# Differential attention: the difference of the two probability maps is made before the turning and the value product

## The reference, cut to what matters

```python
    def attend_block(args):
        qb, b_idx = args
        q_pos = b_idx * Q_BLOCK + jnp.arange(Q_BLOCK)
        logits = jnp.einsum('bhmqd,bhmkd->bhmqk', qb, k).astype(jnp.float32)
        bias = table[t5_bucket_3(key_pos[None, :] - q_pos[:, None])]
        logits = logits + jnp.transpose(bias, (2, 0, 1))[None, :, None]
        visible = key_chunk[None, :] <= (q_pos // CHUNK)[:, None]
        logits = jnp.where(visible, logits, -jnp.inf)
        p = jax.nn.softmax(logits, axis=-1)
        w = p[:, :, 0] - lam * p[:, :, 1]
        return jnp.einsum('bhqk,bhkv->bhqv', w.astype(v.dtype), v)
...
    o = rms_norm_3(o, out_norm_g) * (1.0 - lam_init)
    return o.reshape(B, S, H * 2 * d)
```

## Time and profile before

| | us |
|---|---|
| median of 3 runs | 2302.87 |
| lowest, highest | 2302.66, 2303.80 |
| the profiled execution's own time | 2307.78 |
| its span in the profile | 2306.0 |
| TensorE busy in the span | 1948.8 (85%) |
| VectorE busy | 622.1 (27%) |
| ScalarE busy | 289.0 (13%) |
| GpSimd busy | 101.6 (4%) |

### The profile page before, as it was taken

How to read it: one execution, slowest core, us unless ns; L and a number is a source line. 1 busy time by engine, 2 the same in 40 slices (tenths; PEclk the granted TensorE clock), 3 DMA queues, 4 the chain that set the end, 5 groups by cost and what they waited for, 6 DMA issues and landing times.

```text
span 2306.0 us, 30479 instructions
## 1 busy us (share of the span) xinstructions
PE 1948.8 (85%) x12705; PEld 1147.9 (50%) x12705; DVE 622.1 (27%) x1708; ACT 289.0 (13%) x742; POOL 101.6 (4%) x164
## 2 busy tenths in 40 slices
PE   8999999898655665799966566669999999999999
PEld 4455557554222222486533223224668854548874
DVE  3643583531000000122200000013625411334430
ACT  1123412421000000101100000001500001300000
POOL 0200002300000000000000000002200000010000
PEclk9999999999888888899987877879999999999999
DMA  9968395249999999975999999998234444324420
GB/s 357 386 248 318 121 360 199 64 177 414 425 426 426 426 426 426 370 221 212 380 425 427 426 426 427 425 416 283 72 111 152 164 141 146 110 74 156 163 101 18
DMA packets 194047, 636.81 MB, mean 276 GB/s; under 512 B 7473, under 2 KB 92737, under 8 KB 161448
## 3 DMA queue, kind: packets, MB, share of 16 engines
q1 hardware_dynamic: 187072, 623.78, 69.8%
q0 software_dynamic: 2528, 6.99, 0.9%
q10 hardware_dynamic: 4360, 4.83, 0.7%
HBM read 632.15 MB, written 1.09 MB: 275 GB/s over the span
## 4 chain that ended last, share of the span: by engine, by line
PE 65%; DMA 33%; DVE 1%; ACT 1%; issue 1%; POOL 0%; SPq 0%; DVEq 0%; ACTq 0%; POOLq 0%
DMA ring<-in_moe_w_down 32%; PE bank L713 17%; PE bank L696 17%; PE bank L2826 7%; PE bank L2287 4%; PE bank L1203 3%; PE bank L798 2%; PE bank L2478 1%; PE bank L2271 1%; PE bank L2189 1%; PE bank L2782 1%; PE bank L764 1%; PE bank L789 1%; PE bank L1094 1%; PE bank L610 1%; PE bank L1666 1%
## 5 line engine op out<-in xcount | busy, mean ns | idle before, releaser
L2271 PE MATMUL bank<-ring,arena 128*32 128x256 f32 x3968 | 306.8, 465 | 178.9 <-DMA ring<-in_moe_w_up 114.4
L2271 PEld LDWEIGHTS bank<-ring,arena 128*32 128x32 f32 x3968 | 140.0, 129 | 332.9 <-DMA ring<-in_moe_w_up 148.1
L696 PE MATMUL bank<-ring,hT 128*128 128x512 f32 (+2 forms) x704 | 296.1, 578 | 4.1 <-DVE hT L2466 2.9
L713 PE MATMUL bank<-xn,ring 128*128 128x256 f32 x1280 | 276.6, 379 | 0.0
L713 PEld LDWEIGHTS bank<-xn,ring 128*128 128x128 f32 x1280 | 243.2, 190 | 33.1
L2287 PE MATMUL bank<-ring,arena 128*32 128x256 f32 x1984 | 158.7, 475 | 84.1 <-DMA ring<-in_moe_w_down 73.0
L696 PEld LDWEIGHTS bank<-ring,hT 128*128 128x128 f32 x704 | 132.7, 191 | 154.2 <-issue 149.3
L2826 PE MATMUL bank<-ring,arena 128*128 128x512 f32 x352 | 151.6, 592 | 0.0
L2287 PEld LDWEIGHTS bank<-ring,arena 128*32 128x32 f32 x1984 | 71.8, 131 | 157.0 <-DMA ring<-in_moe_w_down 88.6
L2080 DVE TENSOR_TENSOR arena<-arena,bank 128x256 f32<-128x256 f32 x32 | 13.5, 421 | 491.8 <-ACT arena L2141 491.8
L713 PE MATMUL bank<-hT,ring 128*128 128x256 f32 x512 | 114.4, 386 | 2.0 <-ACT hT L2352 2.0
(11 more groups left out here) (445 smaller groups left out, 1828.0 us busy)
## 6 DMA issues: line engine op xcount, KB each, us to landing
ring<-in_moe_w_gate SPq DMA_DIRECT2D x62, 2048.0 KB, 26.4
ring<-in_moe_w_up SPq DMA_DIRECT2D x62, 2048.0 KB, 26.1
ring<-in_moe_w_down SPq DMA_DIRECT2D x62, 2048.0 KB, 26.2
ring<-in_ada_w SPq DMA_DIRECT2D x24, 2048.0 KB, 17.2
ring<-in_w_up SPq DMA_DIRECT2D x44, 1024.0 KB, 7.4
ring<-in_w_in SPq DMA_DIRECT2D x11, 2048.0 KB, 16.8
ring<-in_w_down SPq DMA_DIRECT2D x10, 2048.0 KB, 7.8
ring<-in_w_out SPq DMA_DIRECT2D x6, 2048.0 KB, 15.1
```

Of the source, the lines that this page charges most:

```text
L696: ins = t_.matmul(bank[b][:, 0:n], lhsT(k)[:, P * t:P * t + P], w[:, k, c0:c0 + n], start=(k == 0), stop=(k == kt - 1))
L713: ins = t_.matmul(bank[b][:, 256 * (j % 2):256 * (j % 2) + 256], w[:, k, P * j:P * j + P], rhs[:, k, :], start=(k == order[0]), stop=(k == ...
L2271: ins = t_.matmul(bank[4][32 * j:32 * j + 32, at:at + 256], xs_now[b][:, 4 * (c % 2) + k, :], w(k)[:, 256 * j:256 * j + 256], start=(c % 2 ...
```

## The change

Two units of a head are now handled together, as one pair s of 12. Both exponentials are taken as before. Then VectorE makes the combined map: the reciprocals of both row sums in one instruction (L2969), the second map scaled by its reciprocal and by minus lambda in place (L2971), and the first map scaled by its reciprocal and added to it (L2973). The last two work in SBUF on 128 or 256 columns, and each of the three waits for the one before. TensorE turns only the combined map (L2920) and makes one value product (L2929). ScalarE copies the product to the output with no factor (L2958), where VectorE had two instructions with factors. Four slots for biased scores and exponentials take the place of three. The first tile's sum and norms are hung into steps 9 and 11 to 13 of 14, where they stood in 17 and 20 to 22 of 27. GpSimd's squares wait for ScalarE's output.

```diff
--- before.py
+++ after.py
@@ -876,7 +876,7 @@
                     f = one_over(j) if u["factor"] is None else weight(j)
                     v.wait_ge(*dve_s.after(f"{tag}.r{j}" if u["factor"] is None else f"{tag}.f{j}"))
                     if u["add"]:
-                        v.wait_ge(*dve_s.after(f"{tag}.o{j - 1}" if tag == "diff" else f"{tag}.o{j - 2}"))
+                        v.wait_ge(*dve_s.after(f"{tag}.o{j - 2}"))
                     v.wait_ge(*pe_s.after(f"{tag}.pv{j}"))
                     src = bank[j % 2][:, 0:u["dst"].shape[-1]]
                     if u["add"]:
@@ -2895,11 +2895,97 @@
         diff_ss = [stats[:, at:at + 12] for at in (16, 40, 64)]
         diff_gain = small[:, 384:512]
 
+        DIFF_PAIRS = len(diff_units) // 2
+        diff_p, diff_s = (b[:, :, :].rearrange("p a (b c) -> p (a b) c", c=S) for b in (p_buf, s_buf))
+
+        def difference_pe(before):
+
+
+            t_ = nc.tensor
+            waits(t_, *before)
+            claim(0, 1, 2, 3, 4, 5, 6, 7)
+            for s in range(DIFF_PAIRS + 2):
+                if s < DIFF_PAIRS:
+                    if s >= 2:
+                        t_.wait_ge(*dve_s.after(f"diff.s{2 * s - 3}"))
+                    for i in (2 * s, 2 * s + 1):
+                        u = diff_units[i]
+                        t_.matmul(score_bank(i, FOUR)[:, 0:u["keys"]], u["q"], u["k"], start=True, stop=True).then_inc(*pe_s.signals(f"diff.qk{i}"))
+                if 1 <= s <= DIFF_PAIRS:
+                    g = s - 1
+                    t_.wait_ge(*dve_s.after(f"diff.c{g}"))
+                    if g >= 2:
+                        t_.wait_ge(*act_s.after(f"diff.pt{g - 2}"))
+                    for k in range(diff_units[2 * g]["keys"] // P):
+                        ins = t_.transpose(bank[6 + g % 2][:, P * k:P * k + P], diff_p[:, 2 * (g % 2), P * k:P * k + P], ident)
+                    ins.then_inc(*pe_s.signals(f"diff.T{g}"))
+                if s >= 2:
+                    g = s - 2
+                    t_.wait_ge(*act_s.after(f"diff.pt{g}"))
+                    if g >= 2:
+                        t_.wait_ge(*act_s.after(f"diff.o{g - 2}"))
+                    values = diff_units[2 * g]["v"]
+                    for k, v in enumerate(values):
+                        ins = t_.matmul(bank[g % 2][:, 0:P], pT_buf[:, g % 2, P * k:P * k + P], v, start=(k == 0), stop=(k == len(values) - 1))
+                    ins.then_inc(*pe_s.signals(f"diff.pv{g}"))
+            for g in (DIFF_PAIRS - 2, DIFF_PAIRS - 1):
+                lend(g % 2, (act_s, f"diff.o{g}"))
+                lend(6 + g % 2, (act_s, f"diff.pt{g}"))
+            for b in FOUR:
+                lend(b, (dve_s, f"diff.s{2 * DIFF_PAIRS - 1}"))
+
+        def difference_act():
+            a = nc.scalar
+            for s in range(DIFF_PAIRS + 2):
+                if s < DIFF_PAIRS:
+                    if s >= 2:
+                        a.wait_ge(*pe_s.after(f"diff.T{s - 2}"))
+                    for i in (2 * s, 2 * s + 1):
+                        n = diff_units[i]["keys"]
+                        a.wait_ge(*dve_s.after(f"diff.s{i}"))
+                        a.activation(diff_p[:, i % 4, 0:n], diff_s[:, i % 4, 0:n], ACT.Exp, bias=row_min[:, i:i + 1], scale=-1.0,
+                                     accum_out=row_sum[:, i:i + 1]).then_inc(*act_s.signals(f"diff.p{i}"))
+                if 1 <= s <= DIFF_PAIRS:
+                    g = s - 1
+                    n = diff_units[2 * g]["keys"]
+                    a.wait_ge(*pe_s.after(f"diff.T{g}"))
+                    if g >= 2:
+                        a.wait_ge(*pe_s.after(f"diff.pv{g - 2}"))
+                    a.activation(pT_buf[:, g % 2, 0:n], bank[6 + g % 2][:, 0:n], ACT.Copy).then_inc(*act_s.signals(f"diff.pt{g}"))
+                if s >= 2:
+                    g = s - 2
+                    a.wait_ge(*pe_s.after(f"diff.pv{g}"))
+                    a.activation(diff_units[2 * g]["dst"], bank[g % 2][:, 0:P], ACT.Copy).then_inc(*act_s.signals(f"diff.o{g}"))
+
+        def difference_dve(also):
+            v = nc.vector
+            for s in range(DIFF_PAIRS + 2):
+                if 1 <= s <= DIFF_PAIRS:
+                    g = s - 1
+                    n = diff_units[2 * g]["keys"]
+                    roots_of = stats[:, 96 + 2 * (g % 2):98 + 2 * (g % 2)]
+                    p1, p2 = diff_p[:, 2 * (g % 2), 0:n], diff_p[:, 2 * (g % 2) + 1, 0:n]
+                    v.wait_ge(*act_s.after(f"diff.p{2 * g + 1}"))
+                    v.reciprocal(roots_of, row_sum[:, 2 * g:2 * g + 2]).then_inc(*dve_s.signals())
+                    v.wait_ge(*dve_s.latest())
+                    v.tensor_scalar(p2, p2, roots_of[:, 1:2], minus_lam, ALU.mult, ALU.mult).then_inc(*dve_s.signals())
+                    v.wait_ge(*dve_s.latest())
+                    v.scalar_tensor_tensor(out=p1, in0=p1, scalar=roots_of[:, 0:1], in1=p2, op0=ALU.mult, op1=ALU.add).then_inc(*dve_s.signals(f"diff.c{g}"))
+                if s < DIFF_PAIRS:
+                    for i in (2 * s, 2 * s + 1):
+                        u = diff_units[i]
+                        v.wait_ge(*pe_s.after(f"diff.qk{i}"))
+                        if i >= 4:
+                            v.wait_ge(*act_s.after(f"diff.p{i - 4}"))
+                        v.tensor_tensor_reduce(out=diff_s[:, i % 4, 0:u["keys"]], in0=score_bank(i, FOUR)[:, 0:u["keys"]], in1=u["bias"], scale=1.0,
+                                               scalar=3e38, op0=ALU.add, op1=ALU.min, accum_out=row_min[:, i:i + 1]).then_inc(*dve_s.signals(f"diff.s{i}"))
+                also(s)
+
         def diff_out_pool():
 
             g = nc.gpsimd
             for n, (t, h) in enumerate(itertools.product(range(2), range(6))):
-                g.wait_ge(*dve_s.after(f"diff.o{2 * n + 1}"))
+                g.wait_ge(*act_s.after(f"diff.o{n}"))
                 o = p3[0][:, t, P * h:P * h + P]
                 g.tensor_tensor(xn[:, t, P * h:P * h + P], o, o, ALU.mult).then_inc(*pool_s.signals(*([f"diff sq{t}"] if h == 5 else [])))
                 if h == 5:
@@ -2920,10 +3006,10 @@
                     .then_inc(*dve_s.signals(*([f"diff norm{t}"] if h == 5 else [])))
 
         def diff_beside_dve(step):
-            if step == 17:
+            if step == 9:
                 diff_sums(0)
-            elif step in (20, 21, 22):
-                diff_norm(0, range(2 * (step - 20), 2 * (step - 20) + 2))
+            elif step in (11, 12, 13):
+                diff_norm(0, range(2 * (step - 11), 2 * (step - 11) + 2))
 
         def third_pool():
             g = nc.gpsimd
@@ -2964,7 +3050,7 @@
             a.wait_ge(*dve_s.after("lam sums"))
             a.activation(stats[:, 122:124], stats[:, 120:122], ACT.Exp).then_inc(*act_s.signals("lam exps"))
             turn_evac("dq", diff_items, 0)
-            attention_act("diff", diff_units, scores=FOUR)
+            difference_act()
             for t in range(2):
                 rows_turn_evac(0, t, 0)
             ffn_act(0)
@@ -3035,7 +3121,7 @@
             turn_evac("dq", diff_items, 1)
             v.wait_ge(*dve_s.latest())
             v.wait_ge(*act_s.after("diff3.free0"))
-            attention_dve("diff", diff_units, scores=FOUR, also=diff_beside_dve)
+            difference_dve(diff_beside_dve)
             diff_sums(1)
             rows_turn_evac(0, 0, 1)
             diff_norm(1, range(6))
@@ -3131,7 +3217,7 @@
             await_chunk(t_, "diff3")
             attention_pe("mem0", mem_units[0], scores=TWO, before=turned("mq0", mem_items[0]), also=lambda step: beside_memory_pe("diff3", step))
             turn_pe("dq", diff_items, before=[(dve_s, "diff k")])
-            attention_pe("diff", diff_units, scores=FOUR, before=turned("dq", diff_items) + [(act_s, "diff3.free0")])
+            difference_pe(turned("dq", diff_items) + [(act_s, "diff3.free0")])
             rows_turn_pe(0, 0, [(dve_s, "diff norm0"), (act_s, "mem0.o7")])
             out3(0)
             ffn_pe(0)
```

## The result

| | before | after |
|---|---|---|
| median of 12 runs each, side by side | 2304.82 us | 2311.67 us |
| profiled execution, span | 2306.0 us | 2309.6 us |
| stage: first biased scores to the projection's first matmul | 29.46 us | 34.90 us |
| from there to the end | 635.28 us | 636.62 us |

The ratio is 1.0027, with a 95% interval from 1.0016 to 1.0038: the change costs **6.2 us** (3.7 to 8.8). The forecast was +4.8 us. 2311.67 lies above the range's end of 2310.2, in part because the base was low: the three runs shown beforehand had 2302.87, the twelve of the comparison (those three among them) 2304.82. The two profiled spans differ by only 3.6 us, since the stage began at 1638.08 us in the one and at 1641.26 in the other, although both kernels issue the same instructions up to there. So stages are compared within profiles, and totals by medians.

What follows compares the result with a forecast made beforehand. The prediction took the loop of VectorE and ScalarE to bound the stage: 3.1 us from the loop and tail plus 1.7 for a projection at 1.2 GHz gave +4.8, thus 2307.7 us, range 2305.0 to 2310.2.

Steps and rivals of the forecast that it cites:

- The ring of VectorE and ScalarE: In the attention stage: the two engines take turns once a head, setting its period: 2.08 us (128 keys), 2.63 (256).
- the sum: Added-up step times from first biased scores to the projection's first matmul, putting the projection 3.1 us later.
- the 1.7 us: At the output projection behind the stage: a start at 1.2 GHz was to lose 1.7 us.
- The loop: One head from biased scores to next biased scores: six of 128 keys take 12.48 us, five of 256 take 13.15.
- The last head: From the last head's biased scores to its combined map being ready: 2.72 us.
- The clock: TensorE's clock hardly matters in the loop; the projection starts at 1.2 GHz and loses 1.7 us.
- the tail: From the last combined map to the projection: last turning, value product, output copy, square and norm, 4.25 us.
- Rival C: TensorE stays at 1.2 GHz through the whole stage and exceeds the loop at 256 keys: +6.8 us, chance 0.13.
- Rival D: Exponentials of head g+1 run while head g is combined, so ScalarE bounds the stage: -6.0 us, chance 0.04.
- The rule of the Trainium skill: TensorE's clock falls only after a whole idle stretch without a matmul; the projection stays at 2.4 GHz, +3.1 us.

Runs made afterwards that it cites:

- changed: The kernel with the change described here, against the kernel before: 2311.67 us, ratio 1.0027.
- e_outdve: Against changed: VectorE, not ScalarE, copies each head's product to the output, right behind the biased scores; stage 38.55 us, 3.65 longer.
- e_fold_sq: e_fold with one wait more: GpSimd squares head g's output only after VectorE's combined map of head g+2; 2313.24 us, ratio 1.0023 against the kernel before.
- e_fold: Against changed: one factor per row replaces the second map's scaling, ScalarE multiplies by the first root while copying; 2312.18 us, ratio 1.0021 against the kernel before.
- e_warm: Against changed: spare identity matmuls on TensorE before it waits for each combined map; stage 33.79 us, ratio 1.0017 against the kernel before.
- e_ahead: Against changed: TensorE issues score products one head further ahead, VectorE's order kept; stage 34.56 us.
- e_swap: Against changed: VectorE makes the biased scores of head g+1 ahead of head g's combined map; 2325.43 us, ratio 1.0076 against the kernel before.
- e_ahead_swap: Against changed: VectorE's order of e_swap together with TensorE's score order of e_ahead; 2305.14 us, ratio 0.9997 against the kernel before.

## Why the prediction was off in size and right in kind

**Right: what bounds the stage.** The ring of VectorE and ScalarE is there, TensorE has gaps in it, and ScalarE's copies cost nothing in it. Direction and mechanism hold; by the runs beside each other the difference of +6.2 lies 1.4 from the forecast, whose own +4.8 is inside the interval. That it lies so near is in part luck: the stage grew by 5.44 us where the sum had 3.14, and the 1.7 us that the forecast added behind it did not come in either profile of changed.

**The loop, mis-sized by 0.07 to 0.1.** Reckoned 2.08 and 2.63, measured 2.17 (from the third head on) and 2.70 to 2.73 where no score is late. At 256 keys biased scores to exponential took 0.52 (0.47 in the sum) and difference to biased scores 0.43 (0.40); at 128 keys 0.38 for 0.33 and 0.29 for 0.26. The durations were right: scaling 0.35 and 0.41 (0.34, 0.41; the slip of 0.055 for 0.409 - 0.35 = 0.059 is of no weight), difference 0.48 to 0.51 at 256 keys. What was small were distances from start to start, and two parts of them can be named. The 0.02 to 0.03 behind the difference are GpSimd's square beside it: in the heads without one, in e_outdve and in e_fold_sq the distance is 0.27 and 0.40. The 0.05 ahead of the exponential are missing in the first two heads (0.33, periods of 2.09 and 2.10) and there from the third on, also in e_outdve, where ScalarE has no output copy. From the third head on ScalarE has one more wait ahead of the exponential, for a turning long done; as in e_fold, that the wait is the cause is argued and not shown. From the first to the last biased scores it took 26.41 us in e_warm and e_ahead alike, against 12.48 + 13.15 = 25.63 in the sum: 0.78 us.

**The last head, missed.** From its biased scores to the end of its combined map took 3.09 us (1664.84 to 1667.93), the sum had 2.72. In e_warm it is 3.07, so it is not the clock: the first exponential starts 0.81 us after the biased scores and not 0.52. It is 0.79 to 0.81 in all seven profiles with the changed kernel's order on VectorE and the output copy on ScalarE, and 0.53 in e_outdve, where that copy is on VectorE. Why is not settled.

**The clock, in the wrong place.** This is the step that failed. The forecast let TensorE stand at 2.4 GHz in the loop ("in the loop itself the clock hardly matters") and at 1.2 GHz in the projection. It was the reverse: 0.50 from 1641 to 1664 us, 1.00 at the projection. The fall that the forecast expected in the tail did come, but at about 1668, after TensorE had been idle for 2.24 us ahead of the last turning. So it slowed the tail, and the clock was back at 1.00 before the projection (5.05 us at a mean of 0.66). Two windows rows of changed, the last head and the tail, and then the tail of e_warm:

```profile
1664.84:1667.93 3.09, 0.89 (x6) 0.70 (x6) 2.39 (x10) 1.52 (x6) 0.40 (x1) 1.00 0.01 3
1667.93:1672.98 5.05, 3.85 (x19) 3.65 (x19) 2.60 (x7) 1.54 (x4) 1.48 (x4) 0.66 0.00 0
```
```profile
1674.83:1679.14 4.31, 2.47 (x18) 2.07 (x19) 2.60 (x7) 1.53 (x4) 1.48 (x4) 1.00 0.00 0
```

Rival C had the mechanism of the loop and the tail, at chance 0.13: it gave up to 0.25 in each of five heads and 0.8 in the tail. Late scores cost 0.35 in all, and from the last map to the projection it took 5.05 us against 4.31 in e_warm, 0.74. The warm tail agrees with the forecast's 4.25. C added the projection's 1.7, which did not come. By terms, the stage's +5.44 is the forecast's 3.14, 0.78 for the periods, 0.35 for late scores, 0.37 for the last head and 0.80 for the tail.

**A clock event counted as a cost of the change.** The forecast compared with one profile of the kernel before, whose projection started at 2.4 GHz, and added 1.7 us for a cold start. The second profile of the kernel before starts it cold, and loses just these 1.70 us; neither profile of changed does. So the cold start is no sure part of either kernel, and the whole 1.7 had no place in the difference.

**Rival D, with one condition too few.** D asked for the biased scores of a head ahead of the difference of the one before and priced that at -6.0. With that order on VectorE alone the stage is 16.8 us longer than in the kernel before (e_swap). With TensorE's scores also further ahead it is 1.9 shorter, and with one pass over the map 3.9.

**The rule of the Trainium skill.** By the Trainium skill, in TensorE: Matmul & The Clock Gate, section HAM oscillation, the forecast would have ended at +3.1. The granted clock was lower than that rule lets expect in the stage: it fell at 1641, after a longest idle time of 2.15 us ahead of the first turning, and stayed at 0.50 for 23 us in which TensorE was busy for 18.77. It fell again at 1668 after 2.24 us of idle time.

## What to carry to other kernels

When an operation is moved onto an engine, write down each engine's queue and follow a head's work until it meets itself: here the length of that ring, and not the busy times, was the period. Reordering one queue cuts the ring that runs through it but can close another through a third engine, so each queue has to be followed anew after the edit (changed, e_swap and e_ahead_swap: 34.9, 46.2 and 27.5 us with the same instructions). A saving on one engine has to be followed into the instruction behind it, which may now run beside another engine's access to the same memory. A clock change seen in one profile is a state of that execution until a second profile shows it.

## What the runs showed of the hardware

- VectorE's pass with both operands in SBUF took 0.55 us instead of 0.35 at 128x128 when GpSimd's square started with it (e_fold), and 0.37 when the square had started 0.2 us before (changed). In all eight pairs of e_fold it ended its undisturbed time plus 0.20 us after the square's recorded start; the square took 0.40 there, and 0.43 or 0.44 at 128 keys in changed. The scaling, with one map as operand, took 0.42 instead of 0.35 beside it (e_outdve). The pass with one operand in PSUM was not slowed (421 ns against 418).
- TensorE's granted clock stayed at 0.50 for 23 us in which it was busy for 18.77 (changed), and in the kernel before it came back after 6.5 us of unbroken work. Fillers kept it at 1.00 with 28.98 busy of 33.79 us; the gain in the stage was 1.1 us.
- A copy from PSUM with a factor per row took ScalarE 0.35 us, without one 0.26.
- From the head on where an engine's program has one more wait ahead of an instruction, for something long done, the instruction came later: by 0.05 us on ScalarE (0.33 to 0.38 us at 128 keys, changed) and by 0.07 on VectorE (0.51 to 0.58 and 0.62 to 0.69, e_fold and e_fold_sq). That the wait is the cause is not isolated.
